# RWKV chunk products as 32-row tiles in four row and column groups

## What is computed

```python
def step(S, inp):
    r_t, w_t, k_t, v_t, kk_t, a_t = inp
    sa = jnp.einsum('bhvk,bhk->bhv', S, -kk_t)
    S = (S * w_t[:, :, None, :]
         + sa[..., None] * (kk_t * a_t)[:, :, None, :]
         + v_t[..., None] * k_t[:, :, None, :])
    o = jnp.einsum('bhvk,bhk->bhv', S, r_t)
    return S, o
```

## Time and profile before

| | us |
|---|---|
| median of 3 runs | 3435.7 |
| lowest, highest | 3434.49, 3436.16 |
| the profiled execution | 3424.82 |
| its span (first to last instruction) | 3422.7 |
| PE busy in the span | 3060.1 (89%) |
| DVE busy in the span | 1388.7 (41%) |
| ACT busy in the span | 991.8 (29%) |

### The profile page before, as it was taken

How to read it: one execution, slowest core, us unless ns; L and a number is a source line. 1 busy time by engine, 2 the same in 40 slices (tenths; PEclk the granted TensorE clock), 3 DMA queues, 4 the chain that set the end, 5 groups by cost and what they waited for, 6 DMA issues and landing times.

```text
span 3422.7 us, 43448 instructions
## 1 busy us (share of the span) xinstructions
PE 3060.1 (89%) x17026; PEld 2503.7 (73%) x17026; DVE 1388.7 (41%) x2236; ACT 991.8 (29%) x1578; POOL 1085.1 (32%) x724
## 2 busy tenths in 40 slices
PE   6887899898999899989888887799997978879997
PEld 4665467776885787867788876699996846658886
DVE  5786354402055213031575533550603054355252
ACT  2222343223122353212442211222222224432221
POOL 0332112443331693444321100143432320124443
PEclk9999999999999999999999977899998989989998
DMA  4986011344732693323220001122222200013332
GB/s 136 269 268 211 25 38 55 106 151 145 218 112 86 156 249 111 94 68 97 69 62 14 2 1 31 50 92 87 92 91 65 81 13 1 31 56 98 93 95 78
DMA packets 130693, 324.77 MB, mean 95 GB/s; under 512 B 54096, under 2 KB 54736, under 8 KB 129760
## 3 DMA queue, kind: packets, MB, share of 16 engines
q1 hardware_dynamic: 95904, 221.29, 21.6%
q0 software_dynamic: 30272, 88.88, 9.3%
q10 hardware_dynamic: 4352, 12.25, 0.9%
HBM read 288.38 MB, written 33.95 MB: 94 GB/s over the span
## 4 chain that ended last, share of the span: by engine, by line
PE 70%; DVE 16%; DMA 4%; ACT 3%; POOL 3%; issue 2%; DVEq 0%; ACTq 0%; POOLq 0%
PE ps L237 16%; PE ps L240 16%; PE ps L242 15%; PE ps L247 3%; DMA d_pb<-arena 3%; DVE h L546 2%; PE ps L2270 2%; POOL ring_r L323 1%; PE ps L526 1%; DVE inv L538 1%; PE ps L2281 1%; PE ps L589 1%; PE ps L1820 1%; PE ps L1834 1%; PE ps L1183 1%
## 5 line engine op out<-in xcount | busy, mean ns | idle before, releaser
L323 POOL TENSOR_TENSOR ring_r<-ring,high 128x1024 fp32r<-128x1024 f32 x330 | 834.0, 2527 | 1628.5 <-ACT high L331 1628.3
L237 PE MATMUL ps<-h_hi,high 128*128 128x512 f32 (+1 forms) x2144 | 749.2, 358 | 65.9 <-DVE h_r L551 40.6
L242 PE MATMUL ps<-h_hi,ring_r 128*128 128x512 f32 (+1 forms) x2144 | 674.9, 350 | 0.0
L240 PE MATMUL ps<-h_r,high 128*128 128x512 f32 (+1 forms) x1952 | 660.3, 348 | 0.0
L331 ACT ACTIVATE high<-ring 128x1024 fp32r<-128x1024 f32 x362 | 381.9, 1055 | 611.1 <-PE ps L237 486.3
L237 PEld LDWEIGHTS ps<-h_hi,high 128*128 128x128 f32 x2144 | 411.4, 192 | 146.7 <-issue 71.4
L242 PEld LDWEIGHTS ps<-h_hi,ring_r 128*128 128x128 f32 x2144 | 379.8, 192 | 54.4
L240 PEld LDWEIGHTS ps<-h_r,high 128*128 128x128 f32 x1952 | 376.9, 193 | 42.0 <-issue 1.0
L240 PE MATMUL ps<-f_r,high 128*128 128x264 f32 (+1 forms) x832 | 261.2, 326 | 0.0
L237 PE MATMUL ps<-f_hi,high 128*128 128x264 f32 (+1 forms) x768 | 236.6, 321 | 0.0
L237 PE MATMUL ps<-z_hi,high 128*128 128x512 f32 x488 | 199.1, 408 | 31.0 <-POOL ring_r L323 30.7
(11 more groups left out here) (417 smaller groups left out, 4663.5 us busy)
## 6 DMA issues: line engine op xcount, KB each, us to landing
ring<-in_units SPq DMA_DIRECT2D x402, 512.0 KB, 3.6
d_ca<-arena POOLq DMA_DIRECT2D x16, 640.0 KB, 8.9
arena<-d_ca POOLq DMA_DIRECT2D x16, 640.0 KB, 6.6
arena<-d_q POOLq DMA_DIRECT2D x32, 256.0 KB, 8.1
d_pb<-arena POOLq DMA_DIRECT2D x16, 512.0 KB, 11.1
arena<-d_pb POOLq DMA_DIRECT2D x16, 512.0 KB, 4.0
arena<-d_ca POOLq DMA_DIRECT2D x16, 512.0 KB, 5.2
arena<-d_k POOLq DMA_DIRECT2D x128, 64.0 KB, 4.6
```

The source lines that it names most:

```text
L237: part = mm(acc, hi[:, cols], self.x_hi(k)[:, t0:t0 + tn], start=(k == 0), stop=False)
L240: mm(acc, hi[:, cols], self.x(k)[:, t0:t0 + tn], start=False, stop=False)
L242: ins = mm(acc, w[:, cols], self.x_hi(k)[:, t0:t0 + tn], start=False, stop=(k == self.kt - 1))
L323: eng.tensor_tensor(b.ring_r[:, slot, :], b.ring[:, slot, :], self.high[:, j % 2, :], ALU.subtract).then_inc(b.unit_lo, 1)
```

## The change

Only the 32x32 diagonal blocks of the grams, the powers and `inv` are kept. In `m.gram`, `m.pw` and `m.inv` chunk c lies on partitions 32c to 32c + 31 (R) with 32 columns for each product and head. Each product of four heads (L1820, L1824, L1834, L1839, L1846) becomes 16 matmuls, head by head and chunk by chunk: chunk c's weights and operand lie on rows R and its result on partitions R of the same bank. The five gram products go to banks 4 and 7, 80 matmuls of 64 rows by 32 columns. The masks are 32 columns wide, and two DVE operations of 128x320 cover all five products of four heads. r is written with chunk c in bank c, o with chunk c in bank 4 + c.

The order moves too. The grams wait for `oc_kept` alone; `b_kept` and `a_masked` are waited for ahead of the levels, and `r_kept` ahead of A and B. u is computed in level 0 and copied by ACT after level 1's y. In the chain the next state comes first, pair by pair as DVE has finished each, and o after it. `a`, `bb` and `s` lie elsewhere in the arena.

```diff
+            if not i:
+                pe.wait_ge(self.cleared, 3)
+            for j in range(RW_PAIRS):
+                if i:
+                    pe.wait_ge(self.s_kept, 4 * i - 3 + j)
+                ins = mm(b.ps[:, 5 + i % 2, j * P:(j + 1) * P], m.a[:, j, c, :], m.s[:, i % 2, j, :], start=True, stop=True)
+            ins.then_inc(self.s_in, 1)
             if i:
-                pe.wait_ge(self.s_kept, 4 * i)
                 pe.wait_ge(self.o_kept, i)
-            else:
-                pe.wait_ge(self.cleared, 3)
             for j in range(RW_PAIRS):
                 ins = mm(b.ps[:, 7, j * RW_C:j * RW_C + cn], m.s[:, i % 2, j, :], m.y(j)[:, c0:c0 + cn],
                          start=True, stop=True)
             ins.then_inc(self.o_in, 1)
-            for j in range(RW_PAIRS):
-                ins = mm(b.ps[:, 5 + i % 2, j * P:(j + 1) * P], m.a[:, j, c, :], m.s[:, i % 2, j, :], start=True, stop=True)
-            ins.then_inc(self.s_in, 1)
...
-            nch = self.chunks(tau)
+            nch, cn = self.chunks(tau), min(RW_C, nt)
+            chunks = [(c, slice(RW_C * c, RW_C * c + cn)) for c in range(nch)]
+            heads = [(q, c, R) for q in range(4) for c, R in chunks]
+            sides = [slice(0, RW_N), slice(RW_N, P)]
             if n:
-                pe.wait_ge(self.b_kept, 2 * n)
-                pe.wait_ge(self.a_masked, 2 * n)
-                pe.wait_ge(self.r_kept, n)
                 pe.wait_ge(self.oc_kept, n)
-                for i in range(4):
-                    for odd in range(2):
-                        rows = slice(RW_N * odd, RW_N * odd + RW_N)
-                        al, be, k, r = (x[rows, tok] for x in (m.al(j), m.be(j), m.y(4 + j), m.y(j)))
-                        lhs, rhs = ((al, be), (be, al), (k, al), (be, r))[i]
-                        ins = mm(b.ps[T, 2 * p + odd, i * P:i * P + nt], lhs, rhs, start=True, stop=True)
-                        if i == 3:
-                            ins.then_inc(self.grams, 1)
-
-            for p in range(2):
-                j = 2 * half + p
-                for odd in range(2):
-                    rows = slice(RW_N * odd, RW_N * odd + RW_N)
-                    ins = mm(b.ps[T, 4 + 3 * odd, p * P:p * P + nt], m.y(4 + j)[rows, tok], m.y(j)[rows, tok],
-                             start=True, stop=True)
-                    if p:
-                        ins.then_inc(self.grams, 1)
+                al, be, k, r = m.al(j), m.be(j), m.y(4 + j), m.y(j)
+                for i, (lhs, rhs) in enumerate(((al, be), (be, al), (k, al), (be, r), (k, r))):
+                    for c, R in chunks:
+                        now = slice(t0 + RW_C * c, t0 + RW_C * c + cn)
+                        for odd, rows in enumerate(sides):
+                            at = (5 * p + i) * RW_C
+                            ins = mm(b.ps[R, 4 + 3 * odd, at:at + cn], lhs[rows, now], rhs[rows, now], start=True, stop=True)
+            ins.then_inc(self.grams, 1)
...
-            pe.wait_ge(self.masked, 4 * n + 4)
+            pe.wait_ge(self.masked, 2 * n + 2)
+            if n:
+                pe.wait_ge(self.b_kept, 2 * n)
+                pe.wait_ge(self.a_masked, 2 * n)
...
-                for q in range(4):
-                    ins = mm(b.ps[T, 0, q * P:q * P + nt], z(q), y(q), start=True, stop=True)
+                    pe.wait_ge(self.zsq, 3 * n + lvl)
+                for q, c, R in heads:
+                    ins = mm(b.ps[R, 0, q * RW_C:q * RW_C + cn], z(q, R), y(q, R), start=True, stop=True)
                 ins.then_inc(self.squares, 1)
...
+                if lvl == 0:
+                    pe.wait_ge(self.toks, 4 * n + 4)
+                    for q, c, R in heads:
+                        ins = mm(b.ps[R, 3, q * RW_N:(q + 1) * RW_N], m.gram[R, q, 2, 0:cn],
+                                 m.bkv[R, q // 2, 2, sides[q % 2]], start=True, stop=True)
+                    ins.then_inc(self.u_in, 1)
             pe.wait_ge(self.u_kept, n + 1)
             pe.wait_ge(self.inv, 5 * n + 5)
-            pe.wait_ge(self.mk_masked, 2 * n + 2)
-            for q in range(4):
-                ins = mm(b.ps[T, 4, q * P:(q + 1) * P], m.inv[T, q, 0:nt], m.au[T, q, :], start=True, stop=True)
+            for q, c, R in heads:
+                ins = mm(b.ps[R, 4, q * P:(q + 1) * P], m.inv[R, q, 0:cn], m.au[R, q, :], start=True, stop=True)
             ins.then_inc(self.p_in, 1)
             pe.wait_ge(self.p_kept, n + 1)
+            pairs = lambda p: [(c, R, odd, 2 * p + odd, sides[odd]) for c, R in chunks for odd in range(2)]
...
+            for p in range(2):
+                for c, R, odd, q, rows in pairs(p):
+                    ins = mm(b.ps[rows, c, p * RW_C:p * RW_C + cn], m.p[R, 0, q, :], m.gram[R, q, 3, 0:cn],
+                             start=True, stop=True)
+            ins.then_inc(self.r_in, 1)
...
+            for p in range(2):
+                at = slice(p * RW_C, p * RW_C + cn)
+                for c, R, odd, q, rows in pairs(p):
+                    mm(b.ps[rows, 4 + c, at], m.p[R, 1, q, :], m.gram[R, q, 3, 0:cn], start=True, stop=False)
+                for c, R, odd, q, rows in pairs(p):
+                    ins = mm(b.ps[rows, 4 + c, at], m.bkv[R, p, 2, rows], m.gram[R, q, 4, 0:cn], start=False, stop=True)
             ins.then_inc(self.oc_in, 1)
...
+            pe.wait_ge(self.r_kept, n + 1)
...
+                if lvl == 1:
+                    act.wait_ge(self.u_in, n + 1)
+                    f(m.au[T, :, RW_N:P], b.ps[T, 3, 0:4 * RW_N].rearrange("p (q v) -> p q v", q=4),
+                      ACT.Copy).then_inc(self.u_kept, 1)
...
+            dve.wait_ge(self.grams, n + 1)
+            for odd in range(2):
+                tt(m.gram[T, odd:4:2, :, 0:cn],
+                   b.ps[T, 4 + 3 * odd, 0:10 * RW_C].rearrange("p (q i s) -> p q i s", q=2, i=5)[:, :, :, 0:cn],
+                   b.masks[T, :, 0:cn].unsqueeze(1).broadcast_to([nt, 2, 5, cn]), ALU.mult).then_inc(self.masked, 1)
...
-            y4 = m.y4[:, 2 * half:2 * half + 2, t0:t0 + nt]
-            tt(y4, y4, b.ps[:, 5, 0:2 * P].rearrange("p (q t) -> p q t", q=2)[:, :, 0:nt], ALU.add).then_inc(self.r_kept, 1)
+            y4 = m.y4[:, 2 * half:2 * half + 2, t0:t0 + nt].rearrange("p q (c t) -> p q c t", c=nch)
+            tt(y4, y4, self.by_chunk(0, nch, cn), ALU.add).then_inc(self.r_kept, 1)
...
-        m2.gram = take(4, 4 * P).rearrange("p q (i s) -> p q i s", i=4)
-        m2.mk, m2.inv, m2.au = take(4, P), take(4, P), take(4, P)
-        m2.pw = take(4, 4 * P).rearrange("p (l z) (q s) -> p l z q s", l=2, q=4)
+        m2.gram = take(20, RW_C).rearrange("p (q i) s -> p q i s", q=4)
+        m2.inv, m2.au = take(4, RW_C), take(4, P)
+        m2.pw = take(16, RW_C).rearrange("p (l z q) s -> p l z q s", l=2, z=2)
...
+        o_[0] = 20064 + 8 * L2
```

More of the change, by code:

```diff
@@ L1863, in tensor @@
             ins.then_inc(self.oc_in, 1)
-            rows = [slice(RW_C * c, min(RW_C * c + RW_C, nt)) for c in range(nch)]
+            pe.wait_ge(self.r_kept, n + 1)
             for p in range(2):
-                heads = lambda s, c: m.p[rows[c], s, 2 * p:2 * p + 2, :].rearrange("t h k -> t (h k)")
-                for c in range(nch):
-                    mm(b.ps[:, c, p * P:(p + 1) * P], heads(0, c), m.bkv[rows[c], p, 0, :], start=True, stop=True)
-                for c in range(nch):
-                    mm(b.ps[:, c, (2 + p) * P:(3 + p) * P], m.bkv[rows[c], p, 0, :], heads(1, c), start=True, stop=False)
-                for c in range(nch):
-                    ins = mm(b.ps[:, c, (2 + p) * P:(3 + p) * P], m.bkv[rows[c], p, 1, :], m.bkv[rows[c], p, 2, :],
+                both = lambda s, R: m.p[R, s, 2 * p:2 * p + 2, :].rearrange("t h k -> t (h k)")
+                for c, R in chunks:
+                    mm(b.ps[:, c, p * P:(p + 1) * P], both(0, R), m.bkv[R, p, 0, :], start=True, stop=True)
+                for c, R in chunks:
+                    mm(b.ps[:, c, (2 + p) * P:(3 + p) * P], m.bkv[R, p, 0, :], both(1, R), start=True, stop=False)
+                for c, R in chunks:
+                    ins = mm(b.ps[:, c, (2 + p) * P:(3 + p) * P], m.bkv[R, p, 1, :], m.bkv[R, p, 2, :],
@@ L1945, in vector @@
             nch = self.chunks(tau)
[L1946 to L1951 removed]
+            cn = min(RW_C, nt)
+            four = lambda bank: b.ps[T, bank, 0:P].rearrange("p (q s) -> p q s", q=4)[:, :, 0:cn]
+            dve.wait_ge(self.grams, n + 1)
[3 more added lines that the diff above has]
+                   b.masks[T, :, 0:cn].unsqueeze(1).broadcast_to([nt, 2, 5, cn]), ALU.mult).then_inc(self.masked, 1)
+            dve.wait_ge(self.masked, 2 * n + 2)
+            tt(m.inv[T, :, 0:cn], m.gram[T, :, 1, 0:cn], b.ident32[T, 0:cn].unsqueeze(1).broadcast_to([nt, 4, cn]),
                ALU.add).then_inc(self.inv, 1)
[L1953 to L1956 removed]
             for lvl in range(4):
@@ L1964, in vector @@
                 dve.wait_ge(self.inv, 5 * n + lvl + 1)
```

(6 more changed lines are left out.)

67 lines of the change are left out of this document (20 added, 47 removed).

## The result

The changed kernel takes 3401.55 us in the median (9 runs, 3396.13 to 3423.55) against 3431.08 us for the kernel before, measured beside it (9 runs, 3418.21 to 3436.24): ratio of the means 0.9927, 95% interval 0.9905 to 0.995, some 25 us saved (the medians lie 29.5 apart). The forecast was 85, and its range ended at 3388. The profiled execution took 3403.74 us, its span is 3401.6.

A forecast was written before the change was run, and what follows sets the result against it. TensorE was taken to set the pace inside the levels of a serial stage. Four groups x 11.15, three x 9.35, 9.85 for n = 0, minus 3.0, plus 5.6 gave 85 us saved: 3351 us, range 3332 to 3388.

The forecast's parts named there:

- the unknown: How fast TensorE takes small tiles: bounded between 7 and 26 ns a pass, a block in 0.22 to 0.85 us.
- Pace, 7 ns a pass: TensorE's 32-column passes, four tiles at once: 7 ns each, a block in 0.22 us, taken as the lower bound.
- Rival 1: Issue-bound TensorE: 12.8 ns a pass, a block 0.41 us, 20 us lost, 3371 us; chance 0.13 (at 26 ns 0.02).
- Wrong altogether: above 17 us: Sign that the whole forecast fails: groups without chain taking above 17 us at full clock.
- (a): From DVE's L1982 to the levels: grams run beside L1982, masks shorter; 2.45 us instead of 5.19, 2.7 saved.
- (b): Levels without chain, with u now in level 0: 5.1 us instead of 13.01, 7.9 saved.
- (c): Group's end, P, r, o and A/B: r and o shorter, A/B waits for r's add; 0.55 us saved.
- (d): Levels of chain groups: 12.4 us instead of 18.55, 6.1 saved, including about 0.8 us waiting for POOL's addition.
- (e): Pool windows on DVE in n = 0 to 3, ahead of r's add: A/B now waits, 3.0 us lost.
- (f): Groups n = 8 and 9 and the last chain step, at 1.2 GHz: 5.6 us saved.
- Rival 2: Clock falls to 1.2 GHz: 3373 us if only groups without chain, 3405 if all, 3385 taken; chance 0.17.
- Rival 3: Row groups writing one PSUM bank take turns: a block 0.85 us, P 3.6 instead of 0.9, 3446 us; chance 0.06.

The follow-up runs named there:

- e4: Kernel before with full 128x128 blocks kept and only the new order (state product ahead of o, u in level 0): ratio 0.9969, -11 us against before.
- e5: Changed kernel with VectorE transposing 32x32 blocks, one square a level and the inverse in the same matmul, 224 matmuls a group for 368: ratio 0.9817.
- e9: Kernel of e5 plus an extra unused TensorE product in each of the first four levels of groups without chain and the last group: ratio 0.983.
- e3: Changed kernel with the same tiles and sums in fewer, wider matmuls, 304 a group for 368: ratio 0.9866, -21 us against the changed kernel.
- e1: Changed kernel with each square of z computed twice, 48 tile matmuls more a group: ratio 1.0001, +25 us against the changed kernel.
- e2: Changed kernel with squares and inverse products for heads 0 and 1 only, 88 tile matmuls fewer a group: ratio 0.9834, -32 us against the changed kernel.

## Why the prediction was wrong

The direction was right; the time was outside the range, 50 us above the forecast. The step that failed is the one called the unknown: it asked only how fast TensorE *takes* small tiles and not how fast it *gets* them. The sum has no term for the supply of instructions, which then stopped TensorE for some 37 us; and it takes the full clock for groups 0 to 7, of which those without chain stood at 0.66.

- **Pace, 7 ns a pass.** Measured 8.5 ns at full clock, a block in 0.27 us for 0.22: nearly right, and worth about half a microsecond a group. Rival 1 (12.8 ns, a block of 0.41) is not what happened; blocks of 0.42 to 0.45 are there, at 1.2 GHz only. The Trainium skill's floor of 25 ns, cited in the prediction, is not one for the engine, as the prediction said: tiles in different row groups start 8.5 ns apart, four of them in turn, so 34 ns in each.
- **The supply, no term at all.** The prediction had the number (2.6 times the matmuls) as an argument for rival 1 and gave it no price. The page of the kernel before counts the 121 packets of q8; what it costs when one block follows another at once could be seen nowhere, as no stretch before asks for blocks closer than 7.8 us. Four groups without chain were to save 11.15 us each and saved 1.8 together, and group 0 lost 1.6 where 9.85 were to be saved; here lies most of the error. Of the 11 us that group 3 is over its forecast, 5.5 are stops. "Wrong altogether: above 17 us" is what happened, if not at full clock.
- **(a)** 2.45 us forecast; group 4 takes 2.66 (1903.10 to 1905.76), the masks 0.89 for 0.90. Right. Group 3 takes 3.07, with 0.44 of stop in the grams; groups 5 and 7, with 0.9 and 1.1 of stop, 3.5 and 3.7.
- **(b)** 5.1 forecast for 13.01; group 3 takes 12.58 (1882.97 to 1895.55), 5.1 of it in three stops, and from 1887.20 on at 1.2 GHz. This term is lost.
- **(c)** 4.5 forecast; group 4 takes 5.64 (1921.56 to 1927.20), 0.83 of it a stop: 4.8 without. Right but for the stop. In group 3, all at 1.2 GHz and without a stop, it is 7.55, longer than the 5.05 before. Groups 0, 1, 5 and 7 take 7.1 to 7.5 in the same way. The groups with chain take 4.8 to 5.3 at full clock, stops left out. So the lower clock alone costs some 2.4 us at the end of each of these five groups, 12 us together.
- **(d)** 12.4 forecast for 18.55; group 4 takes 15.80 (1905.76 to 1921.56), 2.76 of it stops: 13.0 without. The estimate nearly held, and the stops took nearly half the gain. The chain hides part of the supply, and the clock stays up (0.93 to 0.98), so these groups gained and the others did not. The wait for POOL's addition, 0.8 us in the forecast, is not seen in group 4: the stop of 1.37 us covers it.
- **(e)** 3.0 lost, forecast; A/B wait for the add of r once, 0.7 us. The windows are covered again by a TensorE that is late for another reason.
- **(f)** 5.6 forecast; groups 8 and 9 and the last chain step gained 4.4, 0.9 and 1.3. Right, if shared out otherwise (3.2, 1.5 and 0.9 were forecast): they have no more matmuls than before. A chain step takes 4.3 us for 4.6. e4 shows what was not seen: in its profiled execution the order alone gives group 8 10.7 us, as the clock holds there.
- **Rival 2** was right in kind: the clock falls to 0.66 in the groups without chain and not in those with it. It is not a result of the stops alone, since in e5 they are gone and the clock is as low. In the changed kernel it costs the 12 us of (c) and some of the levels, where it can't be told from the supply; in e5's groups without chain it is about 2 us each (e9), in group 8 some 6 (e4). That its worst case, 3405 us with all groups slow, is near the 3401.55 measured is luck: the groups with chain stood at 0.93 to 0.98, and the stops are not in it.
- **Rival 3** is dead: four row groups that write one bank on different partitions take 0.27 us a block and not 0.85, and P takes 1.07 and not 3.6. The Trainium skill's restriction ("TensorEngine Tiling (Array Packing)", Restrictions and Gotchas) does not show where partitions differ.

In sum, of the 60 us missing: the stops make some 37, the lower clock at the ends of five groups 12, and the rest lies in levels that have both. e3 and e5, which keep the sums and cut the instructions, give 21 and 38 back. The sensitivity falls as they go, from 3.6 us a block (e1) to 2.9 (e2), 2.6 (e3) and 2.0 (e5), probably because the copies and the clock come to bind instead, though each of these carries some 10 us of noise. How much of e3's and e5's gain is the shorter sequence of operations and not the supply was not tried apart.

## What to carry to other kernels

Count instructions, not only columns, when a product is cut into tiles: here a block of 256 TensorE instructions (64 fp32 matmuls) costs at least 3.4 us, so a stretch whose matmuls average less than some 53 ns each waits for its program. Read the "issue" releasers of TensorE together with the packets of the instruction queue, and look for operands that can share weights, or for an engine that can make a second operand without a matmul, before splitting further. Look at the granted clock stage by stage as well: here the groups of small tiles alone fell to 1.2 GHz, and the wider products behind them paid for it.
